# Attention pairs on 64x64 quarters of TensorE's array, with the turn as a product by a diagonal of reciprocal sums

## The chip, the cores and the metric

The kernel runs on one NeuronCore of a Trainium2 chip. Its time is the device time of one execution in microseconds (us). Five engines work from queues of their own and meet at semaphores: TensorE (PE; its weight loads are listed as PEld), VectorE (DVE), ScalarE (ACT), GpSimd (POOL) and SyncE (SP, which issues DMAs). PSUM is the memory that TensorE writes; it has 8 banks of 512 float32 numbers on each of 128 partitions. SBUF holds everything else.

## The reference, cut to what matters

The program is two models of two layers each, one after the other. The first has attention over 512 latent and 256 context tokens: 8 heads in branch A (a window of three blocks of 128 keys, the context keys and a sink), 8 heads in branch B (all 768 keys), and in layer 0 the same 16 heads for the 256 context queries over the context keys. The second has 8 heads of causal attention over 512 tokens beside two recurrent mixers. Every attention is, in float32:

```python
def softmax_with_sink(s, sink_hg):
    """s (..., h, g, q, k) float32; sink_hg (h, g): extra logit with no value, dropped after softmax."""
    sk = jnp.broadcast_to(sink_hg.astype(jnp.float32)[:, :, None, None], s.shape[:-1] + (1,))
    p = jax.nn.softmax(jnp.concatenate([s, sk], axis=-1), axis=-1)
    return p[..., :-1]
...
    def one_block(qblk):
        s = jnp.einsum('bqhgd,bkhd->bhgqk', qblk, kall).astype(jnp.float32) * scale
        p = jax.nn.softmax(s, axis=-1).astype(vall.dtype)
        return jnp.einsum('bhgqk,bkhd->bqhgd', p, vall)
...
        s = (jnp.einsum('bqhd,bkhd->bhqk', qn, k_nope)
             + jnp.einsum('bqhr,bkr->bhqk', qr, k_rope)).astype(jnp.float32) * scale
        q_idx = i * ATTN_BLOCK + jnp.arange(ATTN_BLOCK)
        s = jnp.where(key_idx[None, :] <= q_idx[:, None], s, -jnp.inf)
        pr = jax.nn.softmax(s, axis=-1).astype(v.dtype)
        return jnp.einsum('bhqk,bkhd->bqhd', pr, v)
```

The head dimension of the values is 64 everywhere; that of queries and keys is 64 in the first model and 64 + 32, padded to 128, in the second.

## The kernel before, in words

Nearly all of the time goes to dense projections (line 494); between them stand four calls of `attention(pairs, scale, more)`, one for each layer of each model. A *pair* is one block of 128 queries for two heads, called e = 0 and e = 1, with `keys` keys, that is `keys / 128` tiles. The lists are:

- latent pairs (`pairs1`, 32 in each layer of the first model): A and B alternate, A with 4, 5, 5, 4 tiles for the four query blocks, B always with 6;
- context pairs (16, in layer 0 alone), 2 tiles each, after the latent pairs of the same call;
- causal pairs (`mla`, 16 in each layer of the second model), with 1, 4, 2, 3 tiles in turn. They alone have `wide` set: their scores contract over all 128 rows of the array, while those of the first model contract over 64 rows, head 0 on the lower and head 1 on the upper half.

Each pair goes through a chain of steps on several engines. TensorE makes the scores (`scores`, L1526). VectorE moves them to SBUF with mask or scale and finds the row maximum (`maxima`, L1580 and L1586, with a READ_ACCUMULATOR each). ScalarE takes the exponential in place and sums it (`exponent`, L1625). VectorE inverts the sums (L1593) and multiplies the probabilities by them (L1596), one operation a head. TensorE transposes them tile by tile (`turn`, L1542). ScalarE copies the transposed tiles back over the probabilities (L1613), one copy a head. TensorE multiplies them with the values (`values`, L1553), 64 columns of the array for each head. ScalarE copies the 128x128 result to `y` (L1630), and GpSimd splits it into a high and a low part for the next projection (L1649 and L1650).

There is no scheduler: each engine's order is the loop written out for it. On TensorE step i is `scores(i + 1)`, `turn(i - 1)`, `values(i - 2)`; on VectorE `normalize(i - 1)`, `maxima(i + 1)`; on ScalarE `exponent(i)`, two copies of i - 1, `heads(i - 2)`. Scores over 512 keys use banks 0 to 3 whole, so the next pair's scores wait for both maxima (`clear_of`); pairs of at most 512 keys take turns in two sets of banks. Transposed tiles are in banks 4 to 7, and the result of `values` in the last quarter of bank 7 (`O_AT`). Four slots of `probs` are used in turn. At the end of each call ScalarE and VectorE also split the first two weight units of the next projection (`split_unit`, L456 and L459).

Before the causal blocks stands `rwkv_scan`, whose products (L2389, L2423, L2435, L2473) work on 64x64 quarters of the array already: four quarters in turn at L2389 and L2473, the two diagonal ones at L2423 and L2435. It isn't touched, and the prediction reads its rows.

Of the kernel before, what the change touches and what calls it, by code (L numbers as in the profile page):

```python
# [22 lines left out]
ALU = mybir.AluOpType  # L23
# [290 lines left out]
def build(nc, dram, where, where1, where2, where3, n_units):  # L314
    with ExitStack() as ctx:
# [1162 lines left out]
        scores_in, max_out, exp_out, probs_out = (count(n) for n in ("scores_in", "max_out", "exp_out", "probs_out"))  # L1478
        sink_placed, heads_copied = count("sink_placed"), count("heads_copied")
        turned_in, turned_out, heads_in = (count(n) for n in ("turned_in", "turned_out", "heads_in"))  # L1480
# [5 lines left out]
        def attention(pairs, scale, more=()):  # L1486
# [5 lines left out]
            T_AT, O_AT = 2048, 3584 + 384  # L1492
# [13 lines left out]
            def apart(i):  # L1506

                return pairs[i]["keys"] <= BANK

            def turned_at(i, e):  # L1510
                return T_AT + e * (2 * BANK if apart(i) else T)

            with nc.Block() as block:  # L1513
                @block.tensor
                def _(pe):
                    def scores(i):
                        pair = pairs[i]
                        for e in range(2):
                            if clear_of(i):
                                pe.wait_ge(max_out.sem, max_out.at(2 * (clear_of(i) - 1) + e + 1))  # L1520
                            if pair["wide"] or e:
                                for c in range(len(pair["scores"][0])):
                                    for f in ((e,) if pair["wide"] else (0, 1)):
                                        q, k, at, w = pair["scores"][f][c]
                                        to = scores_at(i, f) + at
                                        mm = pe.matmul(ps[:, to:to + w], q, k, start=True, stop=True)  # L1526
                                if pair["wide"]:
                                    mm.then_inc(scores_in.sem, 1)
                        if not pair["wide"]:
                            mm.then_inc(scores_in.sem, 2)  # L1530
# [27 lines left out]
                    for i in range(n + 2):  # L1558
                        if i + 1 < n:
                            scores(i + 1)  # L1560
                        if 0 <= i - 1 < n:
                            turn(i - 1)
                        if 0 <= i - 2 < n:
                            values(i - 2)

                @block.vector
                def _(dve):
# [22 lines left out]
                    def normalize(j):  # L1590
                        pair, st = pairs[j], stat[:, 8 * (j % 4):8 * (j % 4) + 8]
                        dve.wait_ge(exp_out.sem, exp_out.at(2 * j + 2))
                        chain_v.link(dve, dve.reciprocal(st[:, 4:6], st[:, 4:6]))  # L1593
                        for e in range(2):
                            p = probs[:, j % SLOTS, e, 0:pair["keys"]]
# [1513 lines left out]
```

## Time and profile before

| | |
|---|---|
| median of 3 runs | 3421.84 us (3419.05 to 3422.03) |
| the profiled execution, its own time | 3422.04 us |
| its span from first to last instruction | 3419.9 us |
| granted TensorE clock, mean | 0.991 |
| TensorE busy | 3293.9 us (96%) |
| VectorE / ScalarE / GpSimd busy | 1756.3 (51%) / 1200.4 (35%) / 468.1 us (14%) |
| transposes of the four blocks, L1542 | 896 matmuls, 280 ns each |
| scores, L1526 / values, L1553 | 784 / 1792 matmuls |

A float32 product that isn't a transpose is two instructions in the trace, each with a weight load of its own, so the counts are double what the code says.
### The profile page before, as it was taken

The numbers are of one execution on the slowest core, as the hardware profiler recorded it, in microseconds if no ns is written. First come the engines' busy times: TensorE is split into PE (matmuls) and PEld (weight loads), VectorE is DVE, ScalarE is ACT, GpSimd is POOL, SyncE is SP. The second block draws the span as 40 slices with busy tenths as digits, with TensorE's granted clock in tenths as the row PEclk, the third lists the DMA queues.
The fourth block names the chain that finished last, engine by engine and source line by source line (L and its number), as shares of the span: only waits on it lengthen the run. The fifth ranks groups of instructions, "written<-read, shape, count | busy, mean of one in ns | idle before, by whom it ended". The sixth has DMA issues, their size and how long they took to land. (4 is left out here: it accounts for less than half of the span.)

```text
span 3419.9 us, 49577 instructions
## 1 busy us (share of the span) xinstructions
PE 3293.9 (96%) x20432; PEld 2642.9 (77%) x20432; DVE 1756.3 (51%) x2776; ACT 1200.4 (35%) x1974; POOL 468.1 (14%) x557
## 2 busy tenths in 40 slices
PE   6999999999999999999999999899999998999998
PEld 4887778788888787776887867567888777578886
DVE  5875757654132456754324357654443485644433
ACT  3214862311131222853223333353322323532322
POOL 0211212000000022205300133030000022200000
PEclk9999999999999999999999999999999999999999
DMA  6430013353212122012222321012223220122222
GB/s 235 147 111 20 2 56 136 136 191 136 67 64 68 57 85 68 2 62 90 98 93 93 107 78 51 26 56 92 94 93 105 99 80 3 44 87 97 94 99 80
DMA packets 78265, 290.66 MB, mean 85 GB/s; under 512 B 8672, under 2 KB 9056, under 8 KB 77280
## 3 DMA queue, kind: packets, MB, share of 16 engines
q1 hardware_dynamic: 78048, 287.55, 24.7%
q8 instruction: 163, 2.67, 0.3%
q14 instruction: 54, 0.44, 0.0%
HBM read 285.42 MB, written 2.10 MB: 84 GB/s over the span
## 5 line engine op out<-in xcount | busy, mean ns | idle before, releaser
L459 DVE TENSOR_TENSOR w_low<-ring,w_high 128x1024 fp32r<-128x1024 f32 x418 | 525.8, 1258 | 1351.0 <-ACT w_high L456 1350.3
L494 PE MATMUL ps<-arena_r,w_high 128*128 128x512 f32 x3568 | 1140.8, 385 | 11.2 <-PEq L1513 9.2
L456 ACT ACTIVATE w_high<-ring 128x1024 fp32r<-128x1024 f32 x418 | 443.5, 1061 | 1515.8 <-PE ps L494 1506.7
L494 PEld LDWEIGHTS ps<-arena_r,w_high 128*128 128x128 f32 x3568 | 645.3, 188 | 163.8 <-issue 16.5
L494 PE MATMUL ps<-low,w_high 128*128 128x512 f32 (+1 forms) x2448 | 764.8, 361 | 0.0
L494 PE MATMUL ps<-high,w_high 128*128 128x512 f32 x2368 | 737.7, 362 | 15.4 <-DVE low L992 7.1
L494 PE MATMUL ps<-high,w_low 128*128 128x512 f32 x2368 | 731.1, 359 | 0.0
L494 PE MATMUL ps<-arena_r,w_low 128*128 128x512 f32 (+1 forms) x1456 | 545.0, 387 | 0.0
L494 PEld LDWEIGHTS ps<-high,w_high 128*128 128x128 f32 x2368 | 395.6, 189 | 95.3 <-issue 12.2
L494 PEld LDWEIGHTS ps<-low,w_high 128*128 128x128 f32 x2448 | 411.5, 189 | 74.7 <-issue 1.1
L494 PEld LDWEIGHTS ps<-high,w_low 128*128 128x128 f32 x2368 | 395.6, 189 | 70.4
L494 PEld LDWEIGHTS ps<-arena_r,w_low 128*128 128x128 f32 x1456 | 266.3, 188 | 60.9
L555 POOL TENSOR_TENSOR tmp<-tmp 128x512 f32<-128x512 f32 (+1 forms) x42 | 67.5, 1606 | 1525.2 <-ACT tmp L545 1525.2
L1625 ACT ACTIVATE probs<-probs,stat 128x513 f32<-128x513 f32 (+4 forms) x224 | 159.8, 721 | 6.0 <-DVE stat L1586 4.7
L1526 PE MATMUL ps<-arena 64*128 64x256 f32 (+6 forms) x784 | 141.5, 435 | 13.2 <-DVE stat L1580 4.1
L1613 ACT ACTIVATE probs<-ps 128x512 f32<-128x512 f32 (+3 forms) x224 | 122.0, 597 | 55.2 <-PE ps L1542 54.4
L802 DVE CUSTOM_DVE_ANT_0 arena<-arena 128x1024 f32<-128x1024 f32 x104 | 137.1, 1364 | 0.0
L1542 PE MATMUL ps<-const,probs 128*128 128x128 f32 x896 | 123.2, 280 | 4.8 <-DVE probs L1596 3.5
L494 PE MATMUL ps<-low,w_low 128*128 128x512 f32 x368 | 127.4, 374 | 0.0
L1542 PEld LDWEIGHTS ps<-const,probs 128*128 128x128 f32 x896 | 98.2, 141 | 36.3 <-issue 17.5
L1553 PE MATMUL ps<-probs,arena 128*64 128x128 f32 x1792 | 122.6, 279 | 2.5 <-ACT hL L1630 2.0
L1526 PEld LDWEIGHTS ps<-arena 64*128 64x128 f32 (+1 forms) x784 | 76.9, 190 | 57.3 <-issue 40.7
(353 smaller groups left out, 2897.3 us busy)
## 6 DMA issues: line engine op xcount, KB each, us to landing
ring<-in_weights SPq DMA_DIRECT2D x428, 512.0 KB, 3.3
arena<-in_ada_rows SPq DMA_DIRECT2D x80, 512.0 KB, 3.9
arena<-in_ada SPq DMA_DIRECT2D x16, 512.0 KB, 15.6
arena<-in_cond_rows SPq DMA_DIRECT2D x3, 1024.0 KB, 5.9
xL<-in_x SPq DMA_DIRECT2D x1, 2048.0 KB, 10.1
out<-xL SPq DMA_DIRECT2D x4, 512.0 KB, 2.7
low_f<-in_low_rank SPq DMA_DIRECT2D x3, 512.0 KB, 4.4
const<-in_const SPq DMA_DIRECT2D x1, 1104.0 KB, 5.3
```

The costliest lines, as they stand in the source:

```text
L456: act.activation(w_high[:, slot, :], ring[:, place, :], ACT.Copy).then_inc(unit_high.sem, 1)
L459: dve.tensor_tensor(w_low[:, slot, :], ring[:, place, :], w_high[:, slot, :].bitcast(F32), ALU.subtract).then_inc(unit_free.sem, 1)
L494: mm = pe.matmul(bank(4 * (t % 2) + 2 * p + s, width), w, g.split[k][s][x], start=(n == 0 and m == 0), stop=(n == len(part) - 1 and m == 2))
L555: pool.tensor_tensor(tmp[:, 1, 0:total], tmp[:, 1, 0:total], tmp[:, 0, 0:total], ALU.add).then_inc(squares_sum.sem, 1)
L802: ins = dve.tensor_tensor_reduce(out, self.slots[place], self.vectors[s], 1.0, 0.0, ALU.mult, ALU.add, mod[:, to, s:s + 1])
L1526: mm = pe.matmul(ps[:, to:to + w], q, k, start=True, stop=True)
L1542: mm = pe.transpose(ps[:, to:to + P], probs[:, j % SLOTS, e, m * P:m * P + P], con("ident"))
L1553: mm = pe.matmul(ps[e * HD:e * HD + HD, O_AT:O_AT + P], pair["values"][e][m], probs[:, j % SLOTS, e, m * P:m * P + P], start=(m == 0), sto ...
L1613: act.activation(probs[:, j % SLOTS, e, 0:keys], ps[:, turned_at(j, e):turned_at(j, e) + keys], ACT.Copy).then_inc(turned_out.sem, 1)
L1625: act.activation(part, part, ACT.Exp, bias=st[:, 2 + e:3 + e], scale=-1.0, accum_out=st[:, 4 + e:5 + e]).then_inc(exp_out.sem, 1)
```

## The change

All four attention blocks change, by one function.

- Scores of the first model: each 64x128 product becomes two of 64x64, for the lower and the upper 64 queries. The causal ones stay.
- The normalization of the probabilities goes. `invert` takes the reciprocal of the two sums and makes from them two diagonals of 64x64, one for each head, with one product of a doubled identity (`eye`) by the reciprocals. The turn is then no transpose but a product: the probabilities of 64 queries by 64 keys are the weights, the diagonal is the moving operand, four products a tile and head. The result is transposed and normalized.
- The turned tiles of a head lie in two banks, one for each half of the queries, 64 columns a tile. ScalarE copies head 0 (`turned_s`), VectorE head 1 (`turned_v`), each both halves at once.
- `values` takes the keys in two halves of 64, which are summed apart in banks 6 and 7, and stands ahead of `turn` in TensorE's step. The second head's turn waits for the copy of those sums (`heads_copied`), which are in its banks.
- ScalarE copies both sums (256 columns) into one of four places in `tmp`; GpSimd adds them into `y`, and then splits.

TensorE, in the layer-0 latent pairs, before; a row is a run of equal matmuls: the scores of a B pair, a turn of 6 tiles, values of 4 tiles, then the scores of an A pair, a turn of 5 and values of 6:

```order
L1526 MATMUL ps<-arena 128x512 x2
L1526 MATMUL ps<-arena 128x256 x2
L1542 MATMUL ps<-const,probs 128x128 x12
L1553 MATMUL ps<-probs,arena 64x128 x8
L1526 MATMUL ps<-arena 128x256 x4
L1526 MATMUL ps<-arena 128x128 x2
L1542 MATMUL ps<-const,probs 128x128 x10
L1553 MATMUL ps<-probs,arena 64x128 x12
```

The same place now:

```order
L1541 MATMUL ps<-arena 64x512 x4
L1541 MATMUL ps<-arena 64x256 x4
L1574 MATMUL ps<-probs,arena 64x128 x16
L1559 MATMUL ps<-tmp,probs 64x64 x48
L1541 MATMUL ps<-arena 64x256 x8
L1541 MATMUL ps<-arena 64x128 x4
L1574 MATMUL ps<-probs,arena 64x128 x24
L1559 MATMUL ps<-tmp,probs 64x64 x40
```

The values have moved in front of the turn, so that one run of scores lies between a pair's turn and its values, where a whole step lay before; and there are twice as many scores and values, four times as many turns.

VectorE at the same place before, ISA being the custom operation for the maxima:

```order
L1593 RECIPROCAL stat<-stat 128x2
L1596 TENSOR_SCALAR probs<-probs,stat 128x512 x2
L1580 ISA probs,stat<-ps,const,neg_sink 128x640
L1580 ISA stat 128x1
L1580 ISA probs,stat<-ps,const,neg_sink 128x640
L1580 ISA stat 128x1
L1593 RECIPROCAL stat<-stat 128x2
L1596 TENSOR_SCALAR probs<-probs,stat 128x768 x2
```

And now:

```order
L1615 RECIPROCAL stat<-stat 128x2
L1616 TENSOR_TENSOR tmp<-tmp,stat 128x128
L1602 ISA probs,stat<-ps,const,neg_sink 128x640
L1602 ISA stat 128x1
L1602 ISA probs,stat<-ps,const,neg_sink 128x640
L1602 ISA stat 128x1
L1622 COPY probs<-ps 128x2x4x64
L1615 RECIPROCAL stat<-stat 128x2
L1616 TENSOR_TENSOR tmp<-tmp,stat 128x128
```

Two normalizations of the whole width have gone, a small product and a copy out of PSUM have come, and the copy stands behind the maxima of the next pair.

The diff, cut to its core:

```diff
-            T_AT, O_AT = 2048, 3584 + 384
+            T_AT, O_AT, O_STEP = 4 * BANK, 6 * BANK + 3 * P, BANK
+            quarters = (slice(0, HD), slice(HD, P))
+            PLACES = 4
+            room = tmp[:, :, :].rearrange("p a t -> p (a t)")
+            summands = room[:, 0:PLACES * 2 * P].rearrange("p (n r t) -> p n r t", r=2, t=P)
+            scales = room[:, PLACES * 2 * P:PLACES * 2 * P + 4 * HD].rearrange("p (n e t) -> p n e t", e=2, t=HD)
+            eye = room[:, PLACES * 2 * P + 4 * HD:PLACES * 2 * P + 5 * HD]
...
+            def turned_at(e, r):
+                return T_AT + (2 * e + r) * BANK
+
+            def copied(j, e):
+                keys = pairs[j]["keys"]
+                to = probs[:, j % SLOTS, e, 0:keys].rearrange("p (m r t) -> p r m t", r=2, t=HD)
+                both = ps[:, turned_at(e, 0):turned_at(e, 2)].rearrange("p (r x) -> p r x", r=2)[:, :, 0:keys // 2]
+                return to, both.rearrange("p r (m t) -> p r m t", t=HD)
...
+                        for both in zip(*pair["scores"]):
+                            for e, (q, k, at, w) in enumerate(both):
+                                to = scores_at(i, e) + at
+                                for u in quarters:
+                                    mm = pe.matmul(ps[u, to:to + w], q[:, u], k, start=True, stop=True)
+                        mm.then_inc(scores_in.sem, 2)
...
                     def turn(j):
                         pair = pairs[j]
                         tiles = pair["keys"] // P
+                        pe.wait_ge(scale_made.sem, scale_made.at(j + 1))
                         for e in range(2):
-                            pe.wait_ge(probs_out.sem, probs_out.at(2 * j + e + 1))
                             if j:
-                                pe.wait_ge(turned_out.sem, turned_out.at(2 * j - 1 + e if apart(j) and apart(j - 1) else 2 * j))
+                                taken = (turned_s, turned_v)[e]
+                                pe.wait_ge(taken.sem, taken.at(j))
+                                if e:
+                                    pe.wait_ge(heads_copied.sem, heads_copied.at(j))
                             for m in range(tiles):
-                                to = turned_at(j, e) + m * P
-                                mm = pe.transpose(ps[:, to:to + P], probs[:, j % SLOTS, e, m * P:m * P + P], con("ident"))
+                                for r, rows in enumerate(quarters):
+                                    to = turned_at(e, r) + m * HD
+                                    for c, keys in enumerate(quarters):
+                                        at = m * P + c * HD
+                                        mm = pe.matmul(ps[keys, to:to + HD], probs[rows, j % SLOTS, e, at:at + HD],
+                                                       scales[rows, j % 2, e, :], start=True, stop=True)
                             mm.then_inc(turned_in.sem, 1)
 
                     def values(j):
                         pair = pairs[j]
-                        pe.wait_ge(turned_out.sem, turned_out.at(2 * j + 2))
+                        pe.wait_ge(turned_s.sem, turned_s.at(j + 1))
+                        pe.wait_ge(turned_v.sem, turned_v.at(j + 1))
                         if j:
                             pe.wait_ge(heads_copied.sem, heads_copied.at(j))
                         tiles = pair["keys"] // P
                         for m in range(tiles):
-                            for e in range(2):
-                                mm = pe.matmul(ps[e * HD:e * HD + HD, O_AT:O_AT + P], pair["values"][e][m],
-                                               probs[:, j % SLOTS, e, m * P:m * P + P], start=(m == 0), stop=(m == tiles - 1))
+                            for r, rows in enumerate(quarters):
+                                to = O_AT + r * O_STEP
+                                for e in range(2):
+                                    mm = pe.matmul(ps[quarters[e], to:to + P], pair["values"][e][m][rows],
+                                                   probs[rows, j % SLOTS, e, m * P:m * P + P],
+                                                   start=(m == 0), stop=(m == tiles - 1))
                         mm.then_inc(heads_in.sem, 1)
...
                         if i + 1 < n:
                             scores(i + 1)
+                        if 0 <= i - 2 < n:
+                            values(i - 2)
                         if 0 <= i - 1 < n:
                             turn(i - 1)
-                        if 0 <= i - 2 < n:
-                            values(i - 2)
...
+                    def copy(j):
+                        dve.wait_ge(turned_in.sem, turned_in.at(2 * j + 2))
+                        to, turned = copied(j, 1)
+                        dve.tensor_copy(to, turned).then_inc(turned_v.sem, 1)
...
                         if i == n:
                             split_unit(None, dve, 0, 0, None, 0)
-                            split_unit(None, dve, 1, 1, None, 0)
                         if i + 1 < n:
                             maxima(i + 1)
+                        if i:
+                            copy(i - 1)
+                    split_unit(None, dve, 1, 1, None, 0)
...
+                        both = ps[:, 6 * BANK:8 * BANK].rearrange("p (r x) -> p r x", r=2)[:, :, 3 * P:4 * P]
+                        act.activation(summands[:, j % PLACES], both, ACT.Copy).then_inc(heads_copied.sem, 1)
...
-                        split(pair["y"], *pair["halves"])
+                        chain_g.link(pool, pool.tensor_tensor(pair["y"], summands[:, j % PLACES, 0], summands[:, j % PLACES, 1], ALU.add))
+                        split(pair["y"], *pair["halves"]).then_inc(heads_made.sem, 1)
```

ScalarE's step is now `exponent(i)`, `heads(i - 2)`, `copy(i - 1)`, and VectorE's `invert(i - 1)`, `maxima(i + 1)`, `copy(i - 1)`.

## Rows read from the trace of the kernel before

**Rows 1.** Windows: stretch, its us; busy us per engine; PEclk, DMA share, GB/s

```profile
291.40:429.00 137.60, 133.82 (x1342) 103.11 (x1344) 95.39 (x247) 108.37 (x241) 32.96 (x100) 0.96 0.01 2
429.00:456.00 27.00, 25.23 (x230) 15.79 (x226) 21.48 (x94) 26.73 (x100) 14.57 (x43) 1.00 0.00 1
1351.00:1483.50 132.50, 126.12 (x1312) 98.56 (x1312) 92.57 (x226) 106.19 (x226) 31.97 (x94) 1.00 0.01 2
2223.60:2267.30 43.70, 41.23 (x304) 27.68 (x304) 30.57 (x114) 36.05 (x115) 19.77 (x38) 1.00 0.03 11
458.57:461.98 3.41, 3.41 (x12) 2.85 (x12) 0.00 (x0) 0.00 (x0) 0.00 (x0) 0.50 0.86 305
```

**Rows 2.** Timeline (start, length, engine, line, shapes, count), TensorE, latent pairs

```profile
335.48 1.56 PE L1526 MATMUL ps<-arena 64*128 64x512 f32 x8
336.97 1.53 PE L1542 MATMUL ps<-const,probs 128*128 128x128 f32 x12
339.45 1.36 PE L1526 MATMUL ps<-arena 64*128 64x256 f32 x12
343.44 1.56 PE L1526 MATMUL ps<-arena 64*128 64x512 f32 x8
...
355.60 1.15 PE L1526 MATMUL ps<-arena 64*128 64x128 f32 x12
359.16 1.56 PE L1526 MATMUL ps<-arena 64*128 64x512 f32 x8
```

**Rows 3.** Timeline, TensorE, two following context pairs

```profile
440.09 0.70 PE L1526 MATMUL ps<-arena 64*128 64x256 f32 x4
441.90 0.70 PE L1526 MATMUL ps<-arena 64*128 64x256 f32 x4
```

**Rows 4.** Timeline, TensorE, one round of four causal pairs

```profile
2233.56 1.98 PE L1526 MATMUL ps<-arena 128*128 128x512 f32 x4
...
2243.64 1.55 PE L1526 MATMUL ps<-arena 128*128 128x512 f32 x3
```

**Rows 5.** Timeline, quarter products before the causal blocks and what waits for them

```profile
2103.55 0.68 PE L2389 MATMUL ps<-arena,high_f 64*64 64x64 f32 x32
2104.02 0.44 PE L2389 MATMUL ps<-high_f 64*64 64x64 f32 x16
...
2115.96 0.55 PEld L2435 LDWEIGHTS ps<-work,inverses 64*64 64x64 f32 x16
2116.43 0.55 PEld L2435 LDWEIGHTS ps<-inverses,work 64*64 64x64 f32 x16
2116.70 0.69 DVE L2640 TENSOR_TENSOR inverses<-inverses,ps 128x512 f32<-128x512 f32 x1 [3.74 <-PE ps L2435]
...
2143.02 0.64 PE L2473 MATMUL ps<-end_mix,tmp 64*64 64x128 f32 x14
```

**Rows 6.** Groups by shape: count, busy us, mean ns, idle before; copies out of PSUM

```profile
L2652 DVE COPY high_f<-ps 128x256 f32<-128x256 f32 x4 | 1.7, 419 | 0.0
L2686 DVE COPY high_f<-ps 128x512 f32<-128x512 f32 x1 | 0.7, 692 | 0.6 <-PE ps L2513 0.6
...
L1613 ACT ACTIVATE probs<-ps 128x256 f32<-128x256 f32 x32 | 10.3, 376 | 0.0
```

**Rows 7.** Timeline: from an engine's end to TensorE's restart

```profile
452.54 0.62 DVE L1596 TENSOR_SCALAR probs<-probs,stat 128x256 f32<-128x256 f32 x2
452.95 0.46 PEld L1542 LDWEIGHTS ps<-const,probs 128*128 128x128 f32 x4 [0.61 <-DVE probs L1596]
...
454.37 0.31 ACT L1630 ACTIVATE hC<-ps 128x128 f32<-128x128 f32 x1
454.79 0.45 PEld L1553 LDWEIGHTS ps<-probs,arena 128*64 128x64 f32 x8 [0.80 <-ACT probs L1613]
```

**Rows 8.** Timeline: the end of the attention block of layer 1

```profile
1484.27 0.45 POOL L1650 TENSOR_TENSOR low<-hL,arena_r 128x128 fp32r<-128x128 f32 x1
1485.17 0.19 PEld L494 LDWEIGHTS ps<-arena_r,w_high 128*128 128x128 f32 x1 [1.91 <-issue]
```

More of the change, by code:

```diff
@@ L1504, in sinks @@
                 return sum(pair["sink"] is not None for pair in pairs[:i])
[L1506 to L1511, printed above, removed]
+            def turned_at(e, r):
[5 more added lines that the diff above has]
+                return to, both.rearrange("p r (m t) -> p r m t", t=HD)
             with nc.Block() as block:
@@ L1520, in scores @@
                                 pe.wait_ge(max_out.sem, max_out.at(2 * (clear_of(i) - 1) + e + 1))
[L1521 to L1530, printed above, removed]
+                            if wide:
+                                for q, k, at, w in pair["scores"][e]:
+                                    to = scores_at(i, e) + at
+                                    mm = pe.matmul(ps[:, to:to + w], q, k, start=True, stop=True)
+                                mm.then_inc(scores_in.sem, 1)
+                        if wide:
+                            return
+                        for both in zip(*pair["scores"]):
+                            for e, (q, k, at, w) in enumerate(both):
+                                to = scores_at(i, e) + at
+                                for u in quarters:
+                                    mm = pe.matmul(ps[u, to:to + w], q[:, u], k, start=True, stop=True)
+                        mm.then_inc(scores_in.sem, 2)
                     def turn(j):
@@ L1588, in maxima, with invert @@
                             ins.then_inc(max_out.sem, 1)
-                    def normalize(j):
-                        pair, st = pairs[j], stat[:, 8 * (j % 4):8 * (j % 4) + 8]
+                    def invert(j):
+                        st = stat[:, 8 * (j % 4):8 * (j % 4) + 8]
                         dve.wait_ge(exp_out.sem, exp_out.at(2 * j + 2))
                         chain_v.link(dve, dve.reciprocal(st[:, 4:6], st[:, 4:6]))
-                        for e in range(2):
-                            p = probs[:, j % SLOTS, e, 0:pair["keys"]]
-                            dve.tensor_scalar(p, p, st[:, 4 + e:5 + e], None, ALU.mult).then_inc(probs_out.sem, 1)
+                        dve.tensor_tensor(scales[:, j % 2], eye.unsqueeze(1).to_broadcast([P, 2, HD]),
+                                          st[:, 4:6].unsqueeze(2).to_broadcast([P, 2, HD]), ALU.mult).then_inc(scale_made.sem, 1)
@@ L1598, in _ @@
+                    def copy(j):
+                        dve.wait_ge(turned_in.sem, turned_in.at(2 * j + 2))
+                        to, turned = copied(j, 1)
+                        dve.tensor_copy(to, turned).then_inc(turned_v.sem, 1)
+                    chain_v.link(dve, dve.tensor_tensor(eye, con("ident")[:, 0:HD], con("ident")[:, HD:P], ALU.add))
                     maxima(0)
-                    for i in range(n + 2):
-                        if 0 <= i - 1 < n:
-                            normalize(i - 1)
+                    for i in range(n + 1):
+                        if i:
+                            invert(i - 1)
@@ L1602, in _, with copy @@
                         if i == n:
                             split_unit(None, dve, 0, 0, None, 0)
-                            split_unit(None, dve, 1, 1, None, 0)
                         if i + 1 < n:
                             maxima(i + 1)
+                        if i:
+                            copy(i - 1)
+                    split_unit(None, dve, 1, 1, None, 0)
                 @block.scalar
                 def _(act):
-                    def copy(j, e):
-                        keys = pairs[j]["keys"]
-                        act.wait_ge(turned_in.sem, turned_in.at(2 * j + 1 + e if apart(j) else 2 * j + 2))
-                        act.activation(probs[:, j % SLOTS, e, 0:keys], ps[:, turned_at(j, e):turned_at(j, e) + keys],
-                                       ACT.Copy).then_inc(turned_out.sem, 1)
+                    def copy(j):
+                        act.wait_ge(turned_in.sem, turned_in.at(2 * j + 1))
+                        to, turned = copied(j, 0)
+                        act.activation(to, turned, ACT.Copy).then_inc(turned_s.sem, 1)
```

26 lines of the change are left out of this document (14 added, 12 removed).

## The prediction

> **What bounds the kernel now.** I read the page's busy shares first: TensorE is busy 96% of 3419.9 us. Then the busy time by stretch [rows 1]: the change touches the four attention blocks, 137.6 + 27 us (layer 0), 132.5 us, and twice 43.7 us, 385 us in all. In them TensorE is busy 97, 93 and 94%, ScalarE 79% in the long stretch and 99% in the stretch of context pairs. Then TensorE's timeline. Call one pair's parts S (scores), T (turn) and V (values), and count them in key tiles of 128: a windowed pair A has 4 or 5 tiles, a full pair B has 6. One step of the loop is S, T, V of three different pairs. The reader is to see that a step begins where the last one ends, with no wait [rows 2]: the step S(B) T(B) V(A4) lasts 339.45 - 335.48 = 3.97 us, the step S(A5) T(A5) V(B) 3.99, and S(A4) T(A4) V(B) 359.16 - 355.60 = 3.56. The last two differ by 2 tiles and 0.43 us, so a tile costs about 0.215 in each part, and 16 or 14 tiles leave 0.53 and 0.55: a fixed 0.54 us per step, about 0.18 for each of its three changes of array shape (64x128, 128x128, 128x64). So the latent pairs are bound by TensorE alone, with ScalarE and VectorE working beside it. The context pairs run at 441.90 - 440.09 = 1.81 us [rows 3], set by ScalarE. The causal pairs (tiles 1, 4, 2, 3) repeat every 2243.64 - 2233.56 = 10.08 us [rows 4], TensorE again.
>
> **The change, part by part.**
> *Flow on quarters.* Each quarter product does a quarter of the work and four run at once if they behave as the ones before: 32 passes of 64x64x64 take 2104.02 - 2103.55 = 0.47 us, so the eight of one turned tile take 0.117, against 0.109 for a transpose (half of 0.218); 14 passes over 128 columns end within 0.64 us with 0.27 of the last one's own length, at most 0.114 per four [rows 5], so V stays at 0.218 per tile. S stays at 0.213: a quarter of the array, four times the products. So T gets 0.016 per tile dearer (two heads), S and V the same.
> *Shape changes.* Between two groups of quarter products there is nothing: 16 of them take 2116.43 - 2115.96 = 0.47 us from group to group, what their passes take [rows 5]. In the blocks with 64-row scores all 0.54 us of a step go. In the causal block S keeps the whole array, so two changes of three stay; before there were also only two (S and the transposes are both 128x128). There nothing is gained.
> *By flow alone* a latent couple (a step with A, a step with B; A is 4.5 tiles on average, so 10.5 tiles in each part) takes 10.5 x (0.213 + 0.218 + 0.234) = 6.98 us, against (3.99 + 3.56)/2 + 3.97 + 0.11 = 7.86 (the 0.11: V(A5) instead of V(A4) half the time). That would be 0.88 us less.
>
> *What is late next.* Two waits that had slack lose it, since V now stands ahead of T.
> (a) V(j) needs the copies of T(j), and only one S lies between. VectorE's copy (head 1) starts 2116.70 - 2116.43 = 0.27 us after the products end [rows 5]. It takes 0.42 us for 256 elements and 0.69 for 512 [rows 6], so 0.29, 0.56, 0.83 and 0.97 for 1, 3, 5 and 6 tiles. TensorE goes on 0.06 after VectorE (0.35 into 452.54, to 452.95 [rows 7], with 0.35 for the first of the two operations). So V may start 0.33 + copy after T's end: 1.30 for B, 1.16 and 1.02 for A5 and A4, 0.75 for two tiles. S(A) takes 0.85 or 1.07: V(B) waits. S(B) takes 1.28: V(A) doesn't.
> (b) The second head of T(j+1) waits for the copy of V(j)'s sums, since both use banks 6 and 7; only the first head's turn lies between. ScalarE's copy starts about 0.25 after V ends, has 256 elements now, 0.38 us [rows 6], and releases TensorE 0.11 later (454.37 + 0.31 to 454.79 [rows 7]): 0.74 us. The first head's turn takes 0.117 per tile: 0.12 to 0.58 us below 6 tiles, 0.70 for B. So T's second head always starts 0.74 after V, and T costs 0.74 + 0.117 per tile, not 0.234 per tile.
>
> *Latent couple.* Step with S(A): V(B) starts at 1.30, ends at 2.61, T(A) ends at 3.35 + 0.47 or 0.58 = 3.82 or 3.93, mean 3.87; before 3.78: 0.10 more. Step with S(B): 1.28 + V(A) 0.98 + 0.74 + 0.70 = 3.70; before 4.08: 0.38 less. The couple is 0.28 us shorter, x 32 couples: -9 us. The other engines fit in 3.7 us: VectorE has two maxima, the copy 0.97, a reciprocal and a small product in place of two normalizations; ScalarE one copy less.
> *Context pairs.* 0.75 + V 0.44 + 0.74 + 0.23 = 2.16 us against 1.81, x 15: +5 us. ScalarE sheds a copy there, and the loop of waits takes its place.
> *Causal pairs.* S costs 0.427 per tile there (512 columns at 0.107 per 128), and each of the two shape changes 0.18. The four steps, as S, V, T: S(4) 1.71 + V(2) 0.44 + 0.74 + 0.35; S(2) 0.85 + V(3) 0.65 + 0.74 + 0.12; S(3) 1.28 + V(1) 0.22 + 0.74 + 0.47, each with 0.36 for the changes; and S(1), where V(4) waits for its copy: 1.02 + 0.87 + 0.74 + 0.23. Sum 3.60 + 2.72 + 3.07 + 2.86 = 12.25 against 10.08: +2.17, x 7 (two blocks of four rounds, less the ends): +15 us.
> *Ends of the blocks.* The last two steps have no S. Wait (a) then stands there whole, in up to three places (1.30, 1.02 and 1.30 us in layer 1, 0.75 each among context pairs), where before one full copy stood in the open: 1 to 2 us more per block. GpSimd's sum of the two halves is a third operation of 0.45 between the last copy and the next weight load (0.45 at 1484.27, load at 1485.17 [rows 8]): 0.5 more. Together 2 us, +8 us for four. A longer gap can also drop the granted clock: right after the gap at the end of the first blocks it was 0.50, the 1.2 GHz level, for 3.4 us [rows 1], which costs some 1.7 us; for two more ends and half that chance, +2 us.
> *Not on the path:* the diagonal (one operation of 128x128 per pair, not seen before; by the rows from 0.2 to 0.45 us, I take 0.3) ends about when V does; the one sum of identity halves precedes the first maximum, which waits for S.
> The sum of the terms is -9 + 5 + 15 + 8 + 2 = +21 us on the profiled execution's 3422.04 us, which is the median (3421.84) to 0.2: 3443 us.
>
> **A rule weighed.** The turn's products are 14.7 ns apart in the trace (0.47 us for 32 [rows 5]). The Trainium skill, page "TensorE: Matmul & The Clock Gate" (section "Wait — 56ns, not 53.3ns?"), says that matmuls never start less than about 25 ns apart, however small. By it, as an estimate from that page, a turned tile would take 8 x 25 = 200 ns and the 896 of them 74 us more than by the row, so the whole would come to some 3517 us; the row contradicts it, and I keep the row.
>
> **The rivals.**
> A. *The waits don't bind* (faster side): flow decides everywhere. Latent -0.88 x 32 = -28, context pairs bound by ScalarE or by flow, about -3, causal +1, ends +5: 3397 us. For it: TensorE is the bound now in every latent step. Against: 1.30 us of copy can't lie under 0.85 us of S. 15%.
> B. *Only the wait (a) binds*, the sums' copy is on time. Then a latent couple is (2.61 + 1.05) + (1.28 + 0.98 + 1.40) = 7.32, -17; context pairs 1.66, -2; causal +3; ends +6: 3412 us. It decides if ScalarE's copy of the sums takes no more than 0.5 us from V's end to T. 13%.
> C. *Four quarters don't keep their rate over long rows* (slower): no row shows 64x64 products over 256 or 512 columns at once. If S runs at half rate, 1.12 us more for each of 64 latent pairs and 0.43 for 16: some +75, 3520 us. Against it: at 64 and 128 columns the rate holds. 5%.
> D. *The copies are slower than their rows* (strided halves in two banks, or contention): 0.15 us more in each of (a) and (b) gives up to 0.3 a pair, 112 pairs: +30, 3473 us. 9%.
> Forecast (both waits bind, as worked out): 58%, with its own range 3428 to 3458.
>
> **The numbers.** 0.2% (7 us) is about what a measurement of this kernel can tell from no change. Faster takes A and most of B and a little of the forecast: 0.24. Same takes the rest of B and the forecast's lower tail: 0.12. Slower 0.64. The range has to reach B on one side and most of D on the other: 3404 to 3468 us.
>
> **What would show it.** Right: idle time of TensorE ahead of V(B) in the steps with S(A), released by VectorE's copy, and between T's first and second head, released by ScalarE's copy of the sums, in nearly every step; latent steps of 3.8 to 3.9 and 3.6 to 3.8 us; a causal round of about 12 us; no gap between T and S in the latent steps beyond 0.06. Wrong: a latent couple under 7.4 us, a causal round near 10, context pairs at 1.8; or, for C, passes of 512 columns more than 0.43 us apart per four.

## The result and the profile after

The changed kernel takes 3493.51 us (median of four runs, 3492.8 to 3495.25), the one before 3420.78 us in the same comparison: 1.022 times, 95% interval 1.0206 to 1.023. Forecast were 3443 us, 3404 to 3468. So it is slower, as forecast, but by 73 us where 21 were expected, and outside the range. (One of the five executions of the run with half of the turn below, the profiled one, took 6579.88 us, with the projections' matmuls at 654 ns instead of 386; the time given for it is the middle one of all five, and that kernel was run again for a profile.)

The windows of the four changed blocks come first, to be set beside [rows 1] (stretch, its us; busy us per engine with the count of instructions; granted clock, DMA share, GB/s). They are layer 0's latent pairs, its context pairs, layer 1's latent pairs, and the first causal block:

```profile
291.40:448.00 156.60, 135.56 (x4680) 111.61 (x4681) 95.41 (x239) 92.72 (x202) 42.85 (x130) 0.97 0.02 4
448.00:484.90 36.90, 27.31 (x856) 19.42 (x856) 25.55 (x100) 25.89 (x90) 21.32 (x61) 1.00 0.02 4
1380.00:1537.50 157.50, 131.92 (x4640) 110.36 (x4640) 94.85 (x227) 92.51 (x195) 42.34 (x126) 0.98 0.02 4
2276.50:2331.50 55.00, 44.97 (x1025) 31.74 (x1024) 33.64 (x117) 33.66 (x100) 26.19 (x54) 1.00 0.04 12
```

The reader is to see two things. TensorE is busy 132 to 136 us of some 157 in the latent stretches, where it was busy nearly throughout before, while VectorE and ScalarE are no busier than they were: something holds TensorE back that isn't another engine. And its count of matmuls has gone from about 1,340 to 4,680, with as many weight loads.

From the first scores to the end of GpSimd's last split, layer 0's block grew by 28.6 us (166.2 to 194.8), layer 1's by 25.0 (133.6 to 158.5), each causal block by 9.3 (45.3 to 54.5). That makes 72.1 of the 73.6 us between the two profiled spans; the other 1.5 are spread over the 3,000 us between the blocks. The forecast by the same blocks was +2.5, -2.5 and +9.6. So the causal blocks came out as forecast, and nearly the whole miss of some 50 us lies in the 64 latent pairs.

How long the steps take is read off ScalarE's copies of the sums, one a pair (start, length, engine, line). The first two rows lie 15 couples apart in layer 0's latent pairs, the next two 14 context pairs, the last two three causal rounds. Behind them stand two copies of the kernel before, 15 couples apart:

```profile
306.55 0.38 ACT L1661 ACTIVATE tmp<-ps 128x256 f32<-128x256 f32 x1 [1.84 <-PE ps L1574]
...
443.30 0.38 ACT L1661 ACTIVATE tmp<-ps 128x256 f32<-128x256 f32 x1 [1.20 <-PE ps L1574]
...
449.77 0.38 ACT L1661 ACTIVATE tmp<-ps 128x256 f32<-128x256 f32 x1 [0.67 <-PE ps L1574]
...
482.02 0.38 ACT L1661 ACTIVATE tmp<-ps 128x256 f32<-128x256 f32 x1 [0.69 <-PE ps L1574]
...
2284.59 0.38 ACT L1661 ACTIVATE tmp<-ps 128x256 f32<-128x256 f32 x1 [0.73 <-PE ps L1574]
...
2322.61 0.38 ACT L1661 ACTIVATE tmp<-ps 128x256 f32<-128x256 f32 x1 [1.28 <-PE ps L1574]
```

```profile
308.51 0.29 ACT L1630 ACTIVATE hL<-ps 128x128 f32<-128x128 f32 x1
...
425.16 0.29 ACT L1630 ACTIVATE hL<-ps 128x128 f32<-128x128 f32 x1
```

| | before | forecast | after |
|---|---|---|---|
| latent couple | 7.78 | 7.58 | (443.30 - 306.55) / 15 = 9.12 |
| context pair | 1.79 | 2.16 | (482.02 - 449.77) / 14 = 2.30 |
| causal round | 10.09 | 12.25 | (2322.61 - 2284.59) / 3 = 12.67 |

(Before is from the same copies in its trace, for the couple (425.16 - 308.51) / 15. The couples of the experiments are read in the same way, and their instructions are counted between the two copies.) Next, what TensorE's matmuls waited for (engine, line, cause: us in all, times, longest): first among layer 0's latent pairs (310 to 440 us), then among the context pairs (452 to 482 us):

```profile
PE ps L1559 <- issue: 8.4, 12, 1.4
PE ps L1574 <- issue: 3.6, 12, 0.7
PE ps L1541 <- issue: 2.6, 3, 1.1
```

```profile
PE ps L1559 <- ACT tmp L1661: 4.6, 13, 0.4
PE ps L1574 <- issue: 1.2, 2, 0.6
```

Among the context pairs the second head's turn (L1559) waits for ScalarE's copy of the sums, 13 times in 30 us, once a pair: that is the forecast's wait (b). Among the latent pairs this row is missing, and in its place stands "issue", a wait for nothing that the profile shows. Some stalls are of one kind, as the weight loads between 355 and 377 us tell (each row is the first load after a stall, with the idle time ahead of it):

```profile
355.78 0.41 PEld L1541 LDWEIGHTS ps<-arena 64*64 64x64 f32 x11 [1.60 <-issue]
...
359.82 0.26 PEld L1559 LDWEIGHTS ps<-tmp,probs 64*64 64x64 f32 x11 [0.56 <-issue]
...
368.37 0.83 PEld L1559 LDWEIGHTS ps<-tmp,probs 64*64 64x64 f32 x49 [0.42 <-issue]
...
372.36 0.77 PEld L1559 LDWEIGHTS ps<-tmp,probs 64*64 64x64 f32 x45 [0.57 <-issue]
```

They stop in the middle of a turn or of the scores, where no semaphore is waited for. Windows cut at these stalls, and at those of 364.38 and 376.24 us, show what they have in common (columns as above):

```profile
355.77:359.81 4.04, 3.56 (x126) 3.25 (x127) 1.43 (x4) 1.75 (x5) 0.98 (x3) 1.00 0.03 6
359.81:364.37 4.56, 3.77 (x126) 3.15 (x126) 3.03 (x7) 2.44 (x7) 1.57 (x6) 1.00 0.01 4
364.37:368.37 4.00, 3.45 (x127) 2.97 (x126) 2.66 (x7) 2.07 (x5) 0.15 (x1) 1.00 0.02 4
368.37:372.36 3.99, 3.55 (x126) 3.04 (x126) 2.57 (x6) 2.39 (x6) 1.80 (x6) 1.00 0.02 4
372.36:376.23 3.88, 3.62 (x126) 3.17 (x127) 2.85 (x8) 2.64 (x5) 0.91 (x3) 1.00 0.02 4
```

In each there are 126 or 127 matmuls and as many weight loads; with the three or four waits for semaphores, which aren't counted as busy, 256 instructions to the one. Counted from TensorE's first instruction in the trace, the stalls stand at the 194th or 195th of every 256. Of the 28 stalls of 0.4 us or more in its weight loads between 310 and 440 us, 21 stand there, 17.5 us in all or 1.2 a couple; the other 7 all stand ahead of V, 0.07 us after VectorE's copy. The instruction queue q8 moves packets of 16 KB (3.78 MB / 231). The page's rows for TensorE and for that queue (packets, MB, share), before and then after:

```profile
PE 3293.9 (96%) x20432; PEld 2642.9 (77%) x20432; DVE 1756.3 (51%) x2776; ACT 1200.4 (35%) x1974; POOL 468.1 (14%) x557
...
q8 instruction: 163, 2.67, 0.3%
```

```profile
PE 3311.9 (95%) x29168; PEld 2675.9 (77%) x29168; DVE 1764.7 (51%) x2780; ACT 1162.6 (33%) x1862; POOL 506.7 (15%) x669
...
q8 instruction: 231, 3.78, 0.5%
```

Matmuls and loads grew by 2 x 8736 = 17472 instructions, 68 packets of 256, and the queue shows 68 packets more. So TensorE's instructions come in packets of 256, and in the latent blocks one packet lasts it about 4 us on average (from stall to stall 3.6 to 5.3). A latent couple has 586 of them, 2.29 packets (171 before, 0.67 of one): at 4 us each that is 9.16 us, against 9.12 measured. That is theory F: the supply of instructions bounds the latent pairs.

Not every "issue" is that. Where V follows the scores, its first load (line 1574) is also put down to "issue", though it comes 0.07 us after VectorE's copy ended (365.26 + 0.96 = 366.22, load at 366.29): that is the forecast's wait (a).

```profile
365.26 0.96 DVE L1622 COPY probs<-ps 128x768 f32<-128x768 f32 x1 [1.68 <-PE ps L1559]
...
366.29 1.33 PEld L1574 LDWEIGHTS ps<-probs,arena 64*64 64x64 f32 x48 [0.47 <-issue]
```

### The profile page after: what moved, and what is told of

Its sections match the earlier page's. It is cut to its first block and busy times, and to the rows that moved or that the text cites. A ratio compares the mean times of both kernels' runs of the same rounds, so it can differ in the third digit from the quotient of the medians.

```text
span 3493.5 us, 67157 instructions
## 1 busy us (share of the span) xinstructions
PE 3311.9 (95%) x29168; PEld 2675.9 (77%) x29168; DVE 1764.7 (51%) x2780; ACT 1162.6 (33%) x1862; POOL 506.7 (15%) x669
## 3 DMA queue, kind: packets, MB, share of 16 engines
q8 instruction: 231, 3.78, 0.5%
## 5 line engine op out<-in xcount | busy, mean ns | idle before, releaser
L494 PEld LDWEIGHTS ps<-high,w_high 128*128 128x128 f32 x2368 | 395.6, 189 | 95.6 <-issue 12.1
L1559 PE MATMUL ps<-tmp,probs 64*64 64x64 f32 x7168 | 160.2, 222 | 38.2 <-issue 20.4
L1559 PEld LDWEIGHTS ps<-tmp,probs 64*64 64x64 f32 x7168 | 143.2, 135 | 50.9 <-issue 46.4
L1574 PE MATMUL ps<-probs,arena 64*64 64x128 f32 x3584 | 131.4, 274 | 19.9 <-issue 17.5
L1574 PEld LDWEIGHTS ps<-probs,arena 64*64 64x64 f32 x3584 | 107.0, 133 | 52.7 <-issue 46.6
L1622 DVE COPY probs<-ps 128x512 f32<-128x512 f32 (+3 forms) x112 | 77.3, 690 | 138.7 <-PE ps L1559 138.7
L1541 PE MATMUL ps<-arena 64*64 64x256 f32 (+2 forms) x1344 | 106.4, 416 | 14.4 <-DVE stat L1602 4.5
```

The source lines that it names most:

```text
L494: mm = pe.matmul(bank(4 * (t % 2) + 2 * p + s, width), w, g.split[k][s][x], start=(n == 0 and m == 0), stop=(n == len(part) - 1 and m == 2))
L1541: mm = pe.matmul(ps[u, to:to + w], q[:, u], k, start=True, stop=True)
L1559: mm = pe.matmul(ps[keys, to:to + HD], probs[rows, j % SLOTS, e, at:at + HD], scales[rows, j % 2, e, :], start=True, stop=True)
L1574: mm = pe.matmul(ps[quarters[e], to:to + P], pair["values"][e][m][rows], probs[rows, j % SLOTS, e, m * P:m * P + P], start=(m == 0), stop= ...
L1622: dve.tensor_copy(to, turned).then_inc(turned_v.sem, 1)
```

## The experiments

Theory F stands against W (the waits (a) and (b) alone make the steps longer than forecast) and R (quarter products don't keep their rate). For the scores, the changed kernel's trace speaks against R by itself: four loads for passes of 512 columns start 0.43 us after the four before them, the pace that the prediction gave for rival C:

```profile
360.44 0.24 PEld L1541 LDWEIGHTS ps<-arena 64*64 64x64 f32 x4 [0.18 <-issue]
360.87 0.24 PEld L1541 LDWEIGHTS ps<-arena 64*64 64x64 f32 x4 [0.19 <-issue]
```

**Half the turn.** Only the two diagonal quarter products of each tile; the other two quarters of the turned tile are left out.

```
 for c, keys in enumerate(quarters):
+    if c != r:
+        continue
```

> The changed kernel with only the two diagonal ones of the four quarter products of a turned tile (the other two, and so half of the turned tile, are left out). The waits, the copies and their sizes stay. The flow of the turn stays too: on two diagonal quarters 16 passes took 0.47 us in the trace of before, so a tile still takes 0.117 us. Theory F (instruction supply: TensorE's instructions come in blocks of 256, one block at best every 4 us, and a latent couple now has 587 of them in 9.1 us): the latent couple loses 168 instructions, 419 are left, 6.5 us by supply, less than the 7.6 us of the waits; the couple falls from 9.1 to about 7.6 us and the kernel from 3493 to about 3443. Rival W (the waits and copies are dearer than summed): nothing changes, 3485 to 3495. Rival R (the quarter products flow slower than the rows said when all four run): a gain in proportion to the turn alone, up to 1.2 us a couple, 3455.

Measured: 3452.12 us, 1.0092 times the one before (1.0075 to 1.0109). The same kernel again, once, for the profile:

> The same kernel as the one with half of the turn, for its profile. F: latent steps of about 3.8 us on average (4.55 in the changed kernel), with idle time ahead of V(B) and of the second head's turn put down to VectorE and ScalarE, and idle time put down to issue, after every 256 instructions of TensorE, mostly gone. W: steps of 4.5 us.

Measured: 3448.53 us. The times alone leave R open, for its figure (3455) is as near to the two as F's (3443). The turns with six tiles are the key: the array isn't done with them sooner. One turn's matmuls (start, length, count) after the change, free of stalls (first fence; four more of its 96 matmuls begin in the 0.12 us before), and with half the products (second fence):

```profile
352.50 1.75 PE L1559 MATMUL ps<-tmp,probs 64*64 64x64 f32 x92
```

```profile
366.06 1.69 PE L1561 MATMUL ps<-tmp,probs 64*64 64x64 f32 x48
```

Two quarters at work take as long as four, since each quarter still has one product a tile and head. So this run takes away instructions (586 to 418 per couple), but no time of the array, no copy and no wait. What TensorE's matmuls wait for among the latent pairs, and its first copy and the one 15 couples later:

```profile
PE ps L1576 <- issue: 3.3, 10, 0.7
PE ps L1561 <- ACT tmp L1663: 2.3, 7, 0.4
```

```profile
304.19 0.39 ACT L1663 ACTIVATE tmp<-ps 128x256 f32<-128x256 f32 x1 [1.63 <-PE ps L1576]
...
421.04 0.39 ACT L1663 ACTIVATE tmp<-ps 128x256 f32<-128x256 f32 x1 [1.18 <-PE ps L1576]
```

The stalls within the turn and the scores are gone but for two of 0.4 us, in the scores; wait (b) is back in its row, and what is left of "issue" stands ahead of V. A couple takes 116.85 / 15 = 7.79 us, 1.33 less than with the full turn: 32 x 1.33 = 43 us, and the two kernels differ by 41 to 45. Context pairs and causal rounds, with fewer instructions per us, stay as they were (2.27 and 12.59 us). That tells F from W and R, and this kernel's time is near the forecast: 3448.5 to 3452 against 3443.

**Values split.** The opposite: each product of V in two of 64 queries, so the same columns in twice the instructions.

```
-for e in range(2):
-    mm = pe.matmul(ps[quarters[e], to:to + P], ...)
+for h in range(2):
+    for e in range(2):
+        mm = pe.matmul(ps[quarters[e], to + h * HD:to + h * HD + HD], ...)
```

> The changed kernel with every product of the values cut in two of 64 queries; same result, same array time (twice the passes of half the length), 168 more instructions for a latent couple. F: 755 instructions are 11.8 us a couple by supply, +2.6 us x 32 and 0.3 us for each of 48 short pairs at most: 3580 to 3595. W and R: within 10 us of 3493.

Measured: 3572.89 us, 1.045 (1.0433 to 1.0468), 79 us above the changed kernel. Its waits among the latent pairs (310 to 440 us):

```profile
PE ps L1559 <- issue: 23.7, 18, 1.9
PE ps L1576 <- issue: 9.1, 20, 0.9
```

A couple has 755 instructions and takes 11.65 us in layer 0, 11.25 in layer 1: 3.95 and 3.83 us per 256, as in the changed kernel (3.98 and 4.00). Half the turn needs 4.78 us per 256, so it is not bound by them. F again, and against W and R, which said no change; the time came out 7 us under F's lower figure.

**Whole scores.** The scores on 64x128 as before, so fewer instructions but two changes of array shape more per step.

```
-for u in quarters:
-    mm = pe.matmul(ps[u, to:to + w], q[:, u], k, ...)
+mm = pe.matmul(ps[:, to:to + w], q, k, ...)
```

> The changed kernel with the scores of the first model put back on 64 rows by 128 columns: half the products, 36 instructions less for a latent couple (551), and two changes of array shape more in each step (0.36 us). F: the latent steps are bound by instructions, which the shape changes don't need, so the couple gets up to 0.56 us shorter (-18 us in 32 couples) or stays, and only the 16 context pairs pay about 0.2 us each: 3475 to 3495. W (waits and flow alone): the changes show in the latent steps too, about 0.3 us each, +20 us: 3505 to 3520.

Measured: 3484.8 us, 1.0189 (1.0171 to 1.0206). The added shape changes are paid for and more by 36 instructions less a couple (550, in 8.87 us): inside F's figures (3475 to 3495) and below W's, though only 9 us under the changed kernel. At 4.13 us per 256 instructions supply no longer binds all of it.

**Sums copied twice** (a second, equal copy ahead of the one that is waited for) prices wait (b).

```
+chain_s.link(act, act.activation(summands[:, j % PLACES], both, ACT.Copy))
```

> The changed kernel with ScalarE's copy of the two sums made twice, one after the other, before TensorE is released: about 0.4 to 0.5 us more between a pair's values and the second head's turn of the next pair. If wait (b) binds as in the prediction, each of the 48 context and causal pairs gets 0.4 to 0.5 us longer (+19 to +24 us) and each latent pair as well if nothing else hides it (+26 to +32): W says about 3540. F: in the latent pairs TensorE waits for instructions part of the time, and a wait for the copy is time in which the next block can arrive; so only a part of it shows there: 3512 to 3530. If (b) doesn't bind: 3493.

Measured: 3524.3 us, 1.0301 (1.0284 to 1.0318). Context pairs go from 2.30 to 2.81 us, by a copy and its link (0.38 + 0.12), so (b) sets their pace. Among the latent pairs the wait shows again, beside the stalls of supply:

```profile
PE ps L1559 <- ACT tmp L1662: 9.2, 24, 0.5
PE ps L1559 <- issue: 6.3, 11, 0.9
```

Their couple grew by 0.27 to 0.35 us for two copies of 0.5: most of (b) lies behind the supply of instructions there. The time lies in F's figures (3512 to 3530), not at W's 3540.

**VectorE's copy twice** prices wait (a).

```
+chain_v.link(dve, dve.tensor_copy(to, turned))
```

> The changed kernel with VectorE's copy of the second head made twice, one after the other, before TensorE is released. By wait (a) as summed: context pairs +0.5 to 0.6 us each (+9), causal rounds +1.1 us (+9), and latent couples +1.85 us if only waits bind (+59): W says about 3570. F: a couple has some 1.5 us of waiting for instructions, which overlaps with the longer copies, so the latent part is +15 to +40: 3526 to 3551. If (a) doesn't bind anywhere: 3493.

Measured: 3553.1 us, 1.0389 (1.0372 to 1.0407): 2 us above F's range, 17 below W's figure. Context pairs 2.88 us (+0.58), latent couple 10.31 and 10.53 (+1.2 and +1.4, for two copies of 0.7 to 1.0). So (a) binds as well; one of its two places in a couple, or a part of both, is covered by the supply. How much of each the run doesn't tell.

**The order alone.** The kernel before, with V ahead of T and nothing else.

```
+if 0 <= i - 2 < n:
+    values(i - 2)
 if 0 <= i - 1 < n:
     turn(i - 1)
-if 0 <= i - 2 < n:
-    values(i - 2)
```

> The kernel before with one edit, values ahead of the turn in TensorE's step. Full-array transposes, both copies on ScalarE, no wait of the turn for the sums. By wait (a) the values of B start about 1.3 us after the turn's end, behind 0.85 to 1.07 us of scores and their 0.2 of array change: 0.1 us on average in half of the latent steps, 0.4 us once in a round of causal pairs. Sum +5 to +12 us: 3426 to 3433. All theories say the same here; more than 20 us would say that the order, not the quarters, carries the loss.

Measured: 3463.47 us, 1.0125 (1.0108 to 1.0141): a miss of 30 us, and more than the 20 us that were to say that the order carries the loss. The weight loads' waits (300 to 460 us) and one step:

```profile
PEld ps L1553 <- ACT probs L1613: 25.7, 34, 1.6
```

```profile
350.16 1.53 PE L1542 MATMUL ps<-const,probs 128*128 128x128 f32 x12
...
351.73 1.51 ACT L1613 ACTIVATE probs<-ps 128x768 f32<-128x768 f32 x2 [1.34 <-PE ps L1542]
...
353.52 1.10 PEld L1553 LDWEIGHTS ps<-probs,arena 128*64 128x64 f32 x20 [1.17 <-ACT probs L1613]
```

I had counted on the first head's copy being made during the turn. For pairs of more than four tiles both copies wait for both heads, ScalarE makes them one after the other, and V starts 1.9 us after T's end (353.52 - 351.62, the start of the next scores). That wait comes 34 times in layer 0, and a couple takes 8.72 us. The changed kernel makes the two copies at once, on two engines; with half its turn's instructions the same order takes 7.79, as much as the kernel before. So the order's loss is not in the changed kernel. That the two copies at once are what spares it is read from the two traces; no run changes the copies alone.

**Turn in row halves.** If the array's shape changes are worth taking away and instructions are dear, the transposes should take the scores' shape with as few instructions as can be. The kernel before, where each tile of the latent pairs is transposed as two 64x128 halves, with an inner wait for the bank they share:

```
+for r, rows in enumerate((slice(0, HD), slice(HD, P))):
+    to = turned_at(j, e) + r * T + m * HD
+    mm = pe.transpose(ps[:, to:to + HD], probs[rows, ...], con("ident")[rows, rows])
+continue
```

> The kernel before with one edit for the latent pairs: the turn is two transposes of 64 queries by 128 keys per tile and head, on the two row halves of the array, in two banks, so that scores and turn have the same array shape and one of the three changes of a step goes; B and the 5-tile A wait once inside the second head's turn for the end of the first head's, since both use bank 5. 42 instructions more for a couple (211): no bound of supply. Every theory: -0.18 us for each of some 60 latent steps, +0.1 for the wait in 48 of them, so 3411 to 3418. If the pace of a transpose (0.109 us) is set by the 128 columns that move and not by its weight load, two half transposes at once take half of it, 0.05 us less for each of 672 latent tiles and heads, up to -36 us more, until ScalarE (79% busy) binds: 3380 to 3400.

Measured: 3397.03 us, 0.9931 (0.9912 to 0.9951), 22 us faster than the kernel before in the same comparison (3419.18): the second of the two figures (3380 to 3400), the one for a pace set by the moving columns. One step's scores, its turn of six tiles and the start of the values, of this kernel; then the start of the values after the turn of 336.97 in [rows 2], of the kernel before; and this kernel's copies 15 couples apart:

```profile
370.70 1.56 PE L1532 MATMUL ps<-arena 64*128 64x512 f32 x8
372.10 1.06 PE L1552 MATMUL ps<-const,probs 64*128 64x64 f32 x24
373.08 1.09 PE L1567 MATMUL ps<-probs,arena 128*64 128x128 f32 x16
```

```profile
338.43 1.09 PE L1553 MATMUL ps<-probs,arena 128*64 128x128 f32 x16
```

```profile
304.83 0.29 ACT L1649 ACTIVATE hL<-ps 128x128 f32<-128x128 f32 x1
...
408.25 0.28 ACT L1649 ACTIVATE hL<-ps 128x128 f32<-128x128 f32 x1
```

The couple takes 103.42 / 15 = 6.90 us against 7.78. From scores to turn are 1.40 us instead of 336.97 - 335.48 = 1.49, so the shape change that is gone gave 0.09, not 0.18. From turn to values are 0.98 instead of 1.46: the two halves of a tile run at once, and the pairs of them start 0.061 us apart in the trace where whole transposes start at 0.109. Together 0.57 a step with B, and 0.88 - 0.57 = 0.31 are left for the step with A. Of the 32 x 0.88 = 28 us only 22 show in the time; in the profiled execution the granted clock was 0.50 for 13.65 us at the start of layer 1's block, and its first copy of a result came 3.6 us later after the first scores than in the kernel before (17.7 for 14.0). The couple has 213 instructions a couple, one packet in 8.3 us, and no such stall. What TensorE waits for now is VectorE, a little:

```profile
PE ps L1532 <- DVE stat L1600: 1.4, 6, 0.2
PE ps L1556 <- DVE probs L1610: 0.7, 2, 0.4
```

## Why the prediction was wrong

- **The step that failed is "Latent couple"** (under it "By flow alone"): 7.58 us forecast, 9.12 measured, 32 times: 49 of the 50 us missed. (The sum also took the couple before at 7.86, where the copies give 7.78: 3 us of its -9.) Flow, shape changes and both waits were priced, the number of instructions was not: it goes from 171 to 586 a couple, and no term of the sum, no rival and no side of the range speaks of it. Half the turn, with 418, takes 7.79: without the limit the term would have been 0.2 us a couple, 7 us in all, too low.
- Rival C had the right sign and place for a wrong reason. The quarters keep their rate: 92 products of one turn in 1.75 us, the second head's wait in it, as long as 48 take, and 0.43 us for four passes of 512 columns. What falls behind is what feeds them. Rival D is out too: VectorE's copy of 768 columns took 0.96 us (0.97 summed), ScalarE's of the sums 0.38.
- The sign was in the trace of before. `rwkv_scan` sends quarter products in quantity, and its loads stall for "issue". The row is of the kernel before, from the scan that [rows 5] are from; the stall falls within a run of equal products, and counted from TensorE's first instruction it stands at the 194th of 256, as in the changed kernel:

```profile
2156.65 0.31 PEld L2435 LDWEIGHTS ps<-work,inverses 64*64 64x64 f32 x8 [0.89 <-issue]
```

  I read the pace within its groups, 14.7 ns apart, and took it for a pace that can be kept up. At that pace 128 matmuls and their loads, a packet, are gone in 1.9 us; the next one was there after 4.
- *A rule weighed*: the measurement went against the 25 ns rule of the Trainium skill, page "TensorE: Matmul & The Clock Gate" (section "Wait — 56ns, not 53.3ns?"), again in the turn's groups (92 matmuls in 1.75 us are 19 ns each, the wait (b) between them). The cost that it would have given (74 us on top) is near the 50 that came, but it would stand in every turn, and the trace has it in stalls every 256 instructions.
- The Trainium skill, page "Runtime: NRT & Kernel Launch" (section "Instruction fetch mechanics"), says that instructions come in blocks of 16 KB, 256 to the block, and that fetching is hidden since the engine issues more slowly than blocks arrive. The first half the trace bears out (68 packets for 17472 instructions); the second fails here, where TensorE stalls at the same place of most blocks, with the blocks 3.8 to 4.0 us apart on average.
- **Waits (a) and (b)** were right: both are in the trace, and a copy made longer on either path makes the pairs longer. Forecast "in nearly every step", they show so only where supply leaves them bare: context and causal pairs, and half the turn.
- **Context pairs**: 2.30 for 2.16, +8 us instead of +5. **Causal pairs**: 12.67 for 12.25 a round, and each block grew by 9.3 us for 9.6 with its end: right in size. **Flow of V and S** and the missing shape changes: nothing contradicts the flow, but the one shape change taken away by itself (turn in row halves) gave 0.09 us, half of what was counted; in whole scores it can't be told from the supply.
- **Ends**: couples and context pairs make 42.9 + 8.2 of the 53.5 us by which the first two blocks grew; 2.4 are left for their ends and starts, forecast were 4.
- **Clock**: +2 was forecast. In the two profiled executions, the stretches that follow the four blocks ran at 0.50 for 3.4 us more, 3.4 more, 3.4 more and 3.4 less than before (the last few us of the program aside), and their lengths changed by +0.5, +0.5, +1.1 and -0.6 us: 1.5 in all. It was also 0.50 for 6.83 us at the start of layer 1's block, whose first copy of the sums came 14.1 us after the first scores, where it came after 12.1 (half the turn) and 12.4 (whole scores) at 1.00: some 2 us more, within the 2.4 above. Each is one execution, and where the clock falls differs between the traces.
- The sum as it should have been: latent 32 x 1.34 = +42.9, context +8.2, causal blocks with their ends +18.6, ends and starts of the first two +2.4, between the blocks +1.5: +73.6.

What makes up the 4 us per packet the trace shows in part. The packets of that queue come one at a time: they take 0.9 to 2.1 us each and start no less than 3.27 us apart in any of the traces. In layer 0's latent pairs, where they take 0.93 to 1.44, TensorE goes on 1.19 to 1.50 us after a packet's end where it had stalled, and the next packet starts 1.05 us after that at the earliest; with a packet of 0.93 that is 3.2 us at least, and the usual distance is 3.9. So for more than half of the usual distance no packet is moving. What happens in the two waits, ahead of TensorE's restart and of the next packet, stays open; the kernels differ between 3.83 and 4.00 us where they are bound by it, and no run varied it otherwise.

## What to carry to other kernels

Count instructions per microsecond on the fastest engine beside its flow: here 256 TensorE instructions (128 products with their weight loads) lasted about 4 us on average when they were asked for steadily, so quartering products of 0.1 us bought nothing, however well four quarters run at once. When "issue" stands in the list of waits, cut windows at the stalls and count: if each holds the same number of instructions, here 256, it is supply; if the restart follows another engine's end by some 0.07 us, it is a wait. And if a change saves shape switches, look for the version that saves them with the fewest instructions: two row halves of a transpose brought 22 us here, four quarter products cost 73.

## What the runs showed of the hardware that was not expected

- TensorE used up a packet of 256 instructions in 3.98 and 4.00 us (changed kernel) and 3.95 and 3.83 us (values split), mean over 15 couples, with stalls of 0.4 to 1.6 us (changed kernel) at the same place of the 256, most of them within a group of equal products. Packets start no less than 3.27 us apart in any trace, one after the other.
- Two quarters of the array take as long for a turn as four (1.69 and 1.75 us, 48 and 92 matmuls).
- Two transposes of 64 rows, one on each half of the array, start 0.061 us after the two before them, where those of 128 rows follow each other at 0.109.
- The change of shape between scores (64x128) and turn (128x128) was worth 0.09 us where it was taken away.
